# Interleaving the value projection's first column group with the first modulation, and taking a fifth of its weight blocks in fp32

## The reference, cut to what matters

```python
m = jax.nn.silu(cond) @ w_mod + b_mod       # 2048 -> 6 * 2048: shift1, scale1, gate1, shift2, scale2, gate2
h = x * (1 + scale1) + shift1
z = h @ w_in                                # NA q, k, v (8 heads x 128 each), the MLA latents, k_rope
# neighbourhood attention and latent attention, then @ w_o, LayerNorm, SwiGLU, LayerNorm
```

## Time and profile before

| | us |
|---|---|
| median of 3 runs (lowest, highest) | 2914.55 (2913.25, 2916.18) |
| the profiled execution: its own time | 2915.4 |
| its span in the trace | 2913.8 |
| PE busy in the span | 2818.9 (97%) |
| DVE busy | 1891.7 (65%) |
| ACT busy | 1041.7 (36%) |

### The profile page before, as it was taken

How to read it: one execution, slowest core, us unless ns; L and a number is a source line. 1 busy time by engine, 2 the same in 40 slices (tenths; PEclk the granted TensorE clock), 3 DMA queues, 4 the chain that set the end, 5 groups by cost and what they waited for, 6 DMA issues and landing times.

```text
span 2913.8 us, 42087 instructions
## 1 busy us (share of the span) xinstructions
PE 2818.9 (97%) x15844; PEld 2494.5 (86%) x15844; DVE 1891.7 (65%) x2939; ACT 1041.7 (36%) x1811; POOL 185.4 (6%) x259
## 2 busy tenths in 40 slices
PE   7899999999999998799999999999999999999996
PEld 2679999877888776699999999999999988888885
DVE  8766666586885886866666666666666555424337
ACT  7422333224553112644444444444444312112121
POOL 1121111000001000000000000000000000000005
PEclk9999999999999999799999999999999999999998
DMA  9754333352336543232222222222222535223231
GB/s 382 271 187 155 128 129 127 117 188 66 107 115 230 172 169 121 89 110 100 100 100 97 94 95 99 100 100 100 100 95 95 199 118 175 86 85 139 80 123 72
DMA packets 104568, 379.82 MB, mean 130 GB/s; under 512 B 14014, under 2 KB 14418, under 8 KB 102426
## 3 DMA queue, kind: packets, MB, share of 16 engines
q1 hardware_dynamic: 89088, 317.36, 30.7%
q0 software_dynamic: 14800, 61.06, 5.8%
q10 hardware_dynamic: 586, 0.12, 0.0%
HBM read 346.97 MB, written 33.48 MB: 131 GB/s over the span
## 4 chain that ended last, share of the span: by engine, by line
PE 89%; DVE 6%; DMA 2%; ACT 2%; issue 1%; SPq 0%; ACTq 0%; DVEq 0%
PE ps L1926 15%; PE ps L1928 15%; PE ps L1927 15%; PE ps L2414 12%; PE ps L2416 12%; PE ps L2415 12%; DMA mraw<-in_wstream 2%; PE ps L2125 1%; PE ps L2090 1%; PE ps L2073 1%; DVE ps L1854 1%; DVE mlo L1382 0%; DVE stat L1904 0%; PE ps L2121 0%; DVE tmp L1674 0%
## 5 line engine op out<-in xcount | busy, mean ns | idle before, releaser
L2414 PE MATMUL ps<-actl,ringh 128*128 128x320 f32 x1408 | 435.5, 309 | 3.9 <-DVE ringl L1725 3.9
L2415 PE MATMUL ps<-acth,ringh 128*128 128x320 f32 x1408 | 435.1, 309 | 0.0
L2416 PE MATMUL ps<-actl,ringl 128*128 128x320 f32 x1408 | 435.1, 309 | 0.0
L2414 PE MATMUL ps<-acth,ringh 128*128 128x320 f32 x1056 | 327.1, 310 | 7.7 <-DVE ringl L1725 7.7
L2415 PE MATMUL ps<-actl,ringh 128*128 128x320 f32 x1056 | 326.9, 310 | 0.0
L2416 PE MATMUL ps<-acth,ringl 128*128 128x320 f32 x1056 | 326.9, 310 | 0.0
L1926 PE MATMUL ps<-dwh,fring 128*128 128x512 f32 x820 | 319.4, 390 | 1.0 <-DVE dwl L1829 1.0
L1928 PE MATMUL ps<-dwh,fring 128*128 128x512 f32 x820 | 319.2, 389 | 0.0
L1927 PE MATMUL ps<-dwl,fring 128*128 128x512 f32 x820 | 319.1, 389 | 0.0
L1331 DVE TENSOR_TENSOR wlo<-raw,whi 128x1024 fp32r<-128x1024 f32 x111 | 136.3, 1228 | 238.5 <-ACT whi L900 238.4
L1829 DVE TENSOR_TENSOR dwl<-raw,dwh 128x1024 fp32r<-128x1024 f32 x82 | 100.4, 1224 | 291.7 <-ACT dwh L1297 291.7
(11 more groups left out here) (310 smaller groups left out, 5780.3 us busy)
## 6 DMA issues: line engine op xcount, KB each, us to landing
raw<-in_wstream SPq DMA_DIRECT2D x503, 512.0 KB, 3.3
mraw<-in_wstream SPq DMA_DIRECT2D x64, 512.0 KB, 7.7
fscr<-fst POOLq DMA_DIRECT2D x44, 320.0 KB, 2.4
fst<-fscr SPq DMA_DIRECT2D x21, 640.0 KB, 4.0
acc<-in_xT SPq DMA_DIRECT2D x8, 640.0 KB, 16.0
oscr<-ost POOLq DMA_DIRECT2D x16, 320.0 KB, 2.5
ostage<-oscr POOLq DMA_DIRECT2D x16, 320.0 KB, 4.4
acc<-in_xtok POOLq DMA_DIRECT2D x1, 5120.0 KB, 15.5
```

The costliest lines, as they stand in the source:

```text
L2414: mm(out, ringh[:, s, w], ah, start=first, stop=False, skip_group_check=True)
L2415: mm(out, ringh[:, s, w], al, start=False, stop=False, skip_group_check=True)
L2416: ins = mm(out, ringl[:, s, w], ah, start=False, stop=last, skip_group_check=True)
```

## The change

- **Order of units.** `UNITS` takes the units as shift quarter 0, scale quarter 0, shift quarter 1, and so on. After two units four feature blocks of h can be made; DVE adds biases a quarter at a time (`mod1_part`).
- **Blocks in fp32.** Blocks 17, 21, 25, ... 61 of the 64 (`DIRECT`, 12 of them) get no split. PE multiplies the raw fp32 block with `condz`, an fp32 copy of the conditions padded with zeros to 4 columns: two fp32 matmuls in place of four fp32r ones.
- **Interleaving.** After modulation blocks 25 to 34, 41 to 50 and 57 to 61 PE does one token tile of a value block each (`V_TILES`): blocks 0 to 4 of the first column group, 25 tiles. Block 5 follows the loop, with the turning of unit 7 behind its first tile; blocks 6 and 7 and the second group come as before.
- **Loads.** x and the first 8 value blocks are issued between the modulation blocks (`X_LOAD`, `V_LOAD`). A slot of an fp32 block is reused when PE has used it, that of another when DVE has made its low part.
- **Buffers.** `mraw` has 6 slots in place of 8, `mhi` and `mlo` 3 in place of 4, `modrow` 1 in place of 2; the banks of the modulation are 4 and 5.
- **h on ACT.** The scaling moves from DVE to ACT, which now does four activations per feature block, two into `hh` and two into `pb`; DVE keeps the subtraction.
- **Later.** `V_MODS` puts the 16 `gemv` blocks behind value blocks 7 to 15, two behind most of them. POOL's waits keep their meaning, and a small memset moves behind one of them.

```diff
-V_MODS = [0] * 4 + [1] * 8 + [2] * 4
+V_MODS = [0] * 7 + [1] + [2] * 7 + [1]
...
+UNITS = [0, 4, 1, 5, 2, 6, 3, 7]
+DIRECT = [j for j in range(16, B_V) if j % 4 == 1]
+SPLIT = [j for j in range(B_V) if j not in DIRECT]
+X_LOAD = {8: 0, 11: 1, 24: 2, 27: 3, 40: 4, 43: 5, 56: 6, 59: 7}
+V_LOAD = {14: 0, 17: 1, 30: 2, 33: 3, 46: 4, 49: 5, 60: 6, 62: 7}
+V_SPLIT = {22: 0, 26: 1, 36: 2, 42: 3, 52: 4, 58: 5}
+V_TILES = {25 + 16 * q + x: (2 * q + x // 5, x % 5) for q in range(3) for x in range(10 if q < 2 else 5)}
+def mod_row(j):
+    return 8 * UNITS[j // 8] + j % 8
...
-    order = [("w", n) for n in range(B_V + 2)]
+    order = []
+    for j in range(B_V):
+        if j not in DIRECT:
+            order.append(("w", mod_row(j)))
+        if j in V_SPLIT:
+            order.append(("w", B_V + V_SPLIT[j]))
+    order += [("w", B_V + 6), ("w", B_V + 7)]
     m = 0
-    for b in range(16):
+    for b in range(6, 16):
         order.append(("w", B_V + b + 2))
         order += [("m", m + x) for x in range(V_MODS[b])]
         m += V_MODS[b]
...
-        mraw = sb("mraw", [P, 8, 1024], f32, s0)
-        mhi = sb("mhi", [P, 4, 1024], f32r, s0)
-        mlo = sb("mlo", [P, 4, 1024], f32r, s0)
-        modrow = sb("modrow", [4, 2, 512], f32, s0)
-        selt = sb("selt", [5, 2 + 2 * P], f32, s0)
+        pads0 = sb("pads0", [P, (KD + 12) * T], f32, s0)
+        modrow = sb("modrow", [4, 512], f32, s0)
+        mraw = sb("mraw", [P, 6, 1024], f32, s0)
...
+            def mod_load(j):
+                if j - 6 in DIRECT:
+                    sp.wait_ge(used, used_count(mod_row(j - 6)))
+                elif j >= 6:
+                    sp.wait_ge(lo_ready, POS[("w", mod_row(j - 6))] + 1)
+                sp.dma_start(mraw[:, j % 6, :], wstream[mod_row(j)]).then_inc(mod_loaded[j % 6], 16)
...
+            for j in range(B_V):
+                mod_load(j)
+                if j in X_LOAD:
+                    g = X_LOAD[j]
+                    sp.dma_start(xstage[:, 2 * g:2 * g + 2, :], xT[:, 2 * g:2 * g + 2, :]).then_inc(x_in[g], 16)
+                if j in V_LOAD:
+                    stream_load(B_V + V_LOAD[j])
+            for p in range(B_V + 8, RAW_END):
                 stream_load(p)
...
+            pool.memset(condz[:, :, 2:4], 0.0).then_inc(unit_set, 1)
...
+            def mod_split(j):
+                x = SPLIT.index(j)
+                act.wait_ge(mod_loaded[j % 6], 16 * (j // 6 + 1))
+                if x >= 3:
+                    act.wait_ge(used, used_count(mod_row(SPLIT[x - 3])))
+                nc.scalar.activation(mhi[:, x % 3, :], mraw[:, j % 6, :], ACT.Copy).then_inc(hi_ready, 1)
+            def mod_rows(c):
+                act.wait_ge(used, used_count(mod_row(8 * c + 7)))
+                if c:
+                    act.wait_ge(mod1_psum, c)
+                nc.scalar.activation(modrow[:, :], ps[MOD_BANKS[c % 2]][0:4, :], ACT.Copy).then_inc(modrow_ready, 1)
-                act.wait_ge(h_scaled, k + 1)
-                nc.scalar.activation(hh[:, k, :], pb[:, k % 3, :], ACT.Copy).then_inc(h_hi, 1)
-            for b in range(16):
-                if b < 6:
-                    for k in (range(6) if b == 0 else range(2 * b + 4, 2 * b + 6)):
-                        h_part(k)
-                        if b == 0 and k == 1:
-                            split(None, B_V + 1)
+                act.wait_ge(x_in[k // 2], 16)
+                act.wait_ge(mod1_ready, k // 4 + 1)
+                if k >= 3:
+                    act.wait_ge(h_ready, k - 2)
+                for dst in (hh[:, k, :], pb[:, k % 3, :]):
+                    for o, src, c in ((by_column(dst[:, 0:LAT], True), by_column(xstage[:, k, 0:LAT], False), 0),
+                                      (dst[:, LAT:T], xstage[:, k, LAT:T], 1)):
+                        ins = nc.scalar.activation(o, src, ACT.Identity, scale=mod1[:, KD + k, c:c + 1],
+                                                   bias=mod1[:, k, c:c + 1])
+                ins.then_inc(h_hi, 1)
+            for j in range(B_V):
+                if j not in DIRECT:
+                    mod_split(j)
+                if j % 8 == 2 and j >= 8:
+                    mod_rows(j // 8 - 1)
+                if j in V_SPLIT:
+                    split(None, B_V + V_SPLIT[j])
+                q, x = divmod(j - 22, 16)
+                if 0 <= q < 3 and x < 4:
+                    h_part(4 * q + x)
+            mod_rows(7)
+            split(None, B_V + 6)
+            for k in range(12, KD):
+                h_part(k)
+            split(None, B_V + 7)
+            for b in range(6, 16):
...
+            def mod1_part(q):
+                dve.wait_ge(mod1_psum, 2 * q + 2)
+                if q == 0:
+                    dve.wait_ge(consts_in, 16 * CONSTS)
+                k = slice(4 * q, 4 * q + 4)
+                V.tensor_tensor(mod1[:, k, :], psum1[:, k, :], bc[:, k, :], ALU.add)
+                k = slice(KD + 4 * q, KD + 4 * q + 4)
+                V.scalar_tensor_tensor(out=mod1[:, k, :], in0=psum1[:, k, :], scalar=1.0, in1=bc[:, k, :],
+                                       op0=ALU.add, op1=ALU.add).then_inc(mod1_ready, 1)
...
+            for j in range(B_V):
+                if j not in DIRECT:
+                    mod_split(j)
+                if j in V_SPLIT:
+                    split(None, B_V + V_SPLIT[j])
+                q, x = divmod(j - 21, 16)
+                if q >= 0 and x == 0:
+                    mod1_part(q)
+                if 0 <= q < 3 and 2 <= x < 6:
+                    h_rest(4 * q + x - 2)
+            mod1_part(3)
+            split(None, B_V + 6)
+            for k in range(12, KD):
+                h_rest(k)
+            split(None, B_V + 7)
...
+            def mod_block(j):
+                c, b = divmod(j, 8)
+                bank = MOD_BANKS[c % 2]
+                if b == 0 and c >= 2:
+                    pe.wait_ge(modrow_ready, c - 1)
+                if j in DIRECT:
+                    pe.wait_ge(mod_loaded[j % 6], 16 * (j // 6 + 1))
+                else:
+                    pe.wait_ge(lo_ready, POS[("w", mod_row(j))] + 1)
                 for kk in range(2):
                     w = slice(kk * 512, (kk + 1) * 512)
-                    mm(ps[bank][0:4, :], condw[:, 2 * b + kk, :], hi[:, w], start=(b == 0 and kk == 0), stop=False)
-                    ins = mm(ps[bank][0:4, :], condw[:, 2 * b + kk, :], lo[:, w], start=False, stop=(b == 7 and kk == 1))
+                    if j in DIRECT:
+                        ins = mm(ps[bank][0:4, :], condz[:, 2 * b + kk, :], mraw[:, j % 6, w], start=False, stop=False)
+                    else:
+                        x = SPLIT.index(j) % 3
+                        mm(ps[bank][0:4, :], condw[:, 2 * b + kk, :], mhi[:, x, w], start=(b == 0 and kk == 0), stop=False)
+                        ins = mm(ps[bank][0:4, :], condw[:, 2 * b + kk, :], mlo[x][:, w], start=False,
+                                 stop=(b == 7 and kk == 1))
                 ins.then_inc(used, 1)
...
+            def v_tiles(v, first, end):
+                n = B_V + v
+                if first == 0:
+                    arrived(None, n)
+                    pe.wait_ge(h_ready, 2 * v + 2)
+                ins = tok_block(n, hh, hl, 2 * v, v == 0, False, TOK_BANKS[first:end], tile=range(first, end))
+                if end == TT:
+                    ins.then_inc(used, 1)
+            for j in range(B_V):
+                mod_block(j)
+                if j % 8 == 2 and j >= 8:
+                    turn_rows(j // 8 - 1)
+                if j in V_TILES:
+                    v, t = V_TILES[j]
+                    v_tiles(v, t, t + 1)
+            v_tiles(5, 0, 1)
+            turn_rows(7)
+            v_tiles(5, 1, TT)
```

More of the change, by code:

```diff
@@ L99 @@
 POS = {x: p for p, x in enumerate(ORDER)}
+SPLITS = [n for k, n in ORDER if k == "w"]
+RAWS = [(k, n) for k, n in ORDER if k == "m" or n >= B_V]
+RAW_POS = {x: B_V + p for p, x in enumerate(RAWS)}
+RAW_END = B_V + len(RAWS)
 MOD_SEQ = [x for k, x in ORDER if k == "m"]
@@ L593, in _ @@
         def _(sp):
[L594 to L605, removed]
+            def mod_load(j):
[4 more added lines that the diff above has]
+                sp.dma_start(mraw[:, j % 6, :], wstream[mod_row(j)]).then_inc(mod_loaded[j % 6], 16)
             def stream_load(p):
-                sp.wait_ge(lo_ready, p - 3)
+                if p >= B_V + 4:
+                    sp.wait_ge(lo_ready, POS[RAWS[p - 4 - B_V]] + 1)
                 sp.dma_start(raw[:, p % 4, :], wstream[stream_row(p)]).then_inc(loaded[p % 4], 16)
-            for p in range(B_V + 4, len(ORDER)):
+            for j in range(B_V):
[6 more added lines that the diff above has]
+            for p in range(B_V + 8, RAW_END):
                 stream_load(p)
@@ L617, in gu_load @@
                     if i is None and jj == 0:
-                        sp.wait_ge(lo_ready, max(p for p in range(len(ORDER)) if p % 4 == q) + 1)
```

(53 more changed lines are left out.)

89 lines of the change are left out of this document (33 added, 56 removed).

## The result

| | before | after |
|---|---|---|
| median (lowest, highest), 5 runs each, us | 2914.55 (2913.25, 2916.18) | 2927.24 (2926.60, 2931.63) |
| span of the profiled execution, us | 2913.8 | 2925.6 |
| first copy out of value group 0, us | 152.2 | 163.7 |

The ratio is 1.0043 (95% interval 1.0029 to 1.0056): slower by 12.7 us where 7.0 were forecast. The mechanism and the sign were right, the size was not.

What follows compares the result with a forecast made beforehand. PE was taken as the bound: 137.1 us of work, 7.9 us start and 19.6 us idle end value group 0 at 164.6 against 157.6, so 2914.55 + 7.0 = 2921.6 us; range 2914 to 2929.

Steps and rivals of the forecast that it cites:

- PE's work grows by 12.8 us for fp32: Up to the end of value group 0: 12 fp32 blocks at 2.0 us raise PE's work from 124.3 to 137.1 us.
- The front: Modulation up to the first tile: ACT making h ends block 24 at 52.9 us, 4.2 later than the loads would.
- Landing and gaps: Before the first tile: block 24 lands at 45.3 us; PE gaps before blocks 23 and 24 are 2.2 and 2.0 us.
- the smaller ring: Six modulation slots in place of eight: no cost; bound 0.2 us a block, 5 us over 25 blocks.
- ACT's price: Making h on ACT: 1.8 us per feature block against 0.73 before, bounded by 1.7 to 2.4.
- The clock: Rival, chance 0.15: the clock falls at ACT's gaps before blocks 23 and 24, 1.6 us each; 2923 to 2927 us.
- The second and third burst: Blocks 26 to 63, where ACT makes h again: PE waits 0.5 us and 0.4 us in each round; loop ends at 142.5.
- block 6: Tail after the modulation loop: ACT and DVE have this value block's h ready at 149.9 us, 0.7 ahead of PE.
- PE's idle and half-clock time: PE up to the end of value group 0: 19.6 us idle in the changed kernel, 25.6 idle or at half clock before.
- Behind it: After value group 0: no added cost; DVE keeps up with late gemv at 4 us slack, POOL's later start is hidden.
- The signs of being wrong: First tile before 50 us, fp32 block below 1.5, PE idle beyond 3 between j = 26 and 63, distance growing behind 165.
- The rival that would have made it faster: Rival, chance 0.05: fp32 blocks cost 0.86 us, less than split ones; -6.7 us, 2907.9; a gain only below 1.42 a block.

Runs made afterwards that it cites:

- e4: Changed kernel with 8 small fp32 matmuls, result unused, before modulation blocks 23 and 24 to keep PE busy; ratio 1.0032 to the kernel before, first copy 162.7 us.
- e2: Changed kernel with the scaling of h back on DVE and ACT's part one modulation block later; ratio 1.0013 to the kernel before, first copy 154.8 us.
- e1: Changed kernel with all 64 modulation blocks split, none in fp32; ratio 1.0068 to the kernel before.
- e3: Changed kernel with no fp32 blocks and the scaling of h on DVE; ratio 1.0025 to the kernel before, first copy 159.5 us.
- e6: Changed kernel with 6 fp32 blocks in place of 12, all outside the bursts where ACT makes h; ratio 1.0082 to the kernel before, first copy 174.9 us.

## Why the prediction was right in kind and short in size

- **PE's work grows by 12.8 us for fp32.** Right: 2.0 us a block, measured.
- **The front.** Landing and gaps were right to 0.7 us, the smaller ring shows no cost apart (DMA share 1.01 to 1.03 from 20 to 55 us). ACT's price was not: "the form with scale and strided read isn't in the trace". The form with scale and shift was, at 1171 us in the kernel before, where ACT reads PSUM (ns min/median/max); I took 1.8 us from the copy rows instead, with 1.7 to 2.4 as bounds:

```profile
L1198 ACT ACTIVATE stagef<-ps,mod x16: 759/772/777, 1171.0 to 1194.2; 128x512 f32<-128x512 f32 x16
```

  A feature block costs ACT 2.18 us, not 1.8. At 512 columns the changed kernel's instruction has 0.80 us, at 128 columns 0.48, against 0.63 and 0.27 for the copies: some 0.2 us for each instruction at either length, so it is not the strided read, which only the longer one has.
- **The clock.** I had it as a rival at 0.15, at full 1.6 us; it fell, and cost 1.0 (e4). At full clock, in e4, the first tile starts at 54.8 us where 54.9 were worked out: the earlier landing made up for ACT's price up to there. So the 1.8 us by which the changed kernel's first tile is late are the clock's. Block j = 26 starts 1.5 us late (58.2 for 56.7): 1.0 by the clock, 0.5 by ACT's price, as e4's 57.2 tells.
- **The second and third burst.** The turnings at j = 34, 42, 50 and 58 end at 82.3, 97.8, 119.8 and 135.3 us; by the prediction's terms it would be 80.6, 95.0, 116.8 and 131.2. So each of the two bursts adds 1.1 us. The waits were named at j = 40 and 42; they are 1.0 and 0.7 us long, not 0.5 and 0.4. With h on DVE (e2) they are gone. 1.7 us up to j = 34, 1.1 and 1.1, and 0.6 in the stretches behind the bursts are the 4.5 us by which the first copy (163.7, against 159.2 by my sum) was late. In the 0.6 are 0.1 us more for the first matmul of a tile behind a turning, and 0.2 us before block 6, whose h was forecast to be 0.7 us ahead and is ready at 154.9 us, just after PE is.
- **What this means for the sum.** The term that was too small is PE's idle and half-clock time, 19.6 us by my sum and 24.1 measured (169.1 - 7.9 - 137.1): in the main ACT's price for h, then the clock, which I left out of the sum.
- **Behind it.** Right: +11.5 us at the first copy, +11.8 at the end. The remaining difference to the medians' 12.7 lies within the spread of the runs. POOL still waits 38.5 us for the evacuation (46.0 before), and no late `gemv` shows: group 1 keeps the distance of 11.5 us. The slack for that was worked out wrong, though: seven blocks of 7.0 us with 6.7 of DVE's work leave 2.1 us, not 4.
- **The signs of being wrong.** One of the four came true: listed waits of PE between j = 26 and 63 are 3.5 us in all, where "beyond 3 us" was to count against me. It pointed at the term that was short.
- **The rival that would have made it faster.** It asked for a cheaper fp32 block, and I wrote that such blocks count on DVE and ACT "only where these are late", yet priced that at nothing. That is the term that fails in e1 and e3: PE's list wins when fp32 blocks are taken away, and the bursts on ACT and DVE lose more. The forecast for the changed kernel did not depend on it; its gain "at all below 1.42 us a block" holds no more, because a split block in a burst costs more than its 0.93. The 12.8 us are what PE spends on fp32 blocks, not what the kernel would gain without them: there it loses (e1).

## What to carry to other kernels

Work put into another engine's waits is paid for by the engines that feed it: add up each feeding engine's list over the few blocks of a burst, not over the stage, and take its prices from any line of the trace with the same form. Waits that grow in this way can take the clock down as well (e6). A dearer instruction on the bound engine can be right where its feeders are late and wrong a few blocks on, so place such blocks by bursts and not by a fixed stride. Comparing one early instant in two traces told effects of 1 us apart that the whole run's time, at 0.1%, could not.

## What the runs showed of the hardware

The granted clock fell twice in the changed kernel before the first tile: between 28 and 30 us, after a pause of 1.2 us in which PE did nothing and sparse work before it, and by 50 us, after one of 2.4 and with another under way; the second fall was gone when the gaps were filled with 8 small matmuls each. The first fall in windows of 1 us, columns as before:

```profile
28.00:29.00 1.00, 0.04 (x1) 0.00 (x0) 1.00 (x1) 0.99 (x1) 0.00 (x0) 1.00 1.02 406
29.00:30.00 1.00, 0.90 (x3) 0.30 (x4) 0.95 (x2) 0.78 (x2) 0.00 (x0) 0.51 1.02 406
```

I had expected falls only behind gaps of two microseconds and more, from the one in the kernel before. Nor does the pause decide by itself: e6 has the same idle times listed (1.8 and 1.1 us before its matmuls at 23.8 and 29.2 us, as the changed kernel at 23.7 and 29.1), and the granted clock stays at 1.00 from 16 to 48 us.
